# Down matrix of each expert loaded four neighbouring rows a partition, gate and up products read with a stride of four columns

## The chip, the cores and the metric

The kernel runs on one core of one Trainium2 chip. The metric is the device time of one execution in microseconds (us). Everything is in float32. "The span" is the time from the first to the last instruction of the profiled execution.

## The reference

The kernel computes two blocks one after the other on 256 tokens of width 1024 (272 rows with 16 meta tokens in the first layer). The first block has two layers, and each of these ends in a mixture of experts. That part is what the change touches:

```
def expert_block(args):
    xb, e = args
    hb = jax.nn.silu(xb @ w_gate[e]) * (xb @ w_up[e])
    return hb @ w_down[e]
```

There are 32 experts in each of the two layers; a token goes to two of them. `w_gate[e]` and `w_up[e]` are 1024 x 512, `w_down[e]` is 512 x 1024, so each of the three matrices is 2 MB and an expert is 6 MB. The second block (a state-space mixer, an MLP, attention, a second MLP) is not touched.

## The kernel before

**Experts.** Each layer's mixture of experts (`moe(l)`) runs over all 32 experts in order, with 32 token slots for each. For one expert TensorE does, in this order: `gate_up` (line 722), the weighing-in of the expert before (lines 751 and 755), a transpose of the hidden values (line 916), in some experts a `dispatch` of tokens for the next group of four experts (line 742) and in the first layer some preparation for the state-space mixer, and `down` (line 734). ScalarE applies silu (line 1435) and copies the transposed hidden values (line 1440); VectorE multiplies (line 2005) and copies the result out (line 2011).

**`gate_up`.** The stationary operand is a 128 x 32 slice of the tokens, and the moving operand is the weight. For each of the 8 slices `k` of the width, four matmuls with q = 0..3 write four groups of 32 partitions of one PSUM bank; each streams 256 columns, 128 of gate and 128 of up: columns 128q to 128q+127 of both. The profile counts two instructions for a float32 matmul, so 64 for a `gate_up`, in 16 sets of four. After silu, product and transpose, the 128 x 128 tile `hidT` holds for each q the hidden values of group q, with the hidden index on the partitions.

**`down`.** For each of 4 slices k, `hidT[:, 32k:32k+32]` is stationary, and row slice k of the down matrix is moving, in four column groups. Slice k of the down matrix must hold on partition p the row that belongs to hidden value p of group k: before the change this is row 128k + p.

**Loads.** The weights stream through `ring`, six slots of 16 KB a partition. All loads are issued by the sync engine (SP) in one order written out by hand: the three matrices of an expert after those of the one before, each as soon as its slot is free, which is when `gate_up` or `down` of the expert that held it is done. Two experts are in the ring at a time (slots in two sets of three, `expert_order` says in which order the three go); the third expert of each layer (`EXTRA`) goes to a part of `work`. In `load` (line 463 issues) gate and up are read as `"(p k) n -> p (k n)"`: partition p gets 8 neighbouring rows, one piece of 16 KB. Down is read as `"(q p) n -> p q n"`: partition p gets rows p, 128+p, 256+p, 384+p, four pieces of 4 KB:

```
if kind == "down":
    src = src.rearrange("(q p) n -> p q n", p=P)
else:
    src = src.rearrange("(p k) n -> p (k n)", k=DC)
```

TensorE waits before `gate_up` for the loads of gate and up, and before `down` for that of down. A second pass for overfull experts (`sp.Fori(1, rounds)`) has the same two forms.

**Around it.** Before the first mixture comes the recurrent mixer, between the two the short convolution (projections at lines 673 and 681, rows out at line 699), after the second everything of the second block.

Of the kernel before, what the change touches and what calls it, by code (L numbers as in the profile page):

```python
# [26 lines left out]
P = 128  # L27
D = 1024
DC = D // P
# [43 lines left out]
def first_and_second_block(nc, a, out):  # L73
# [4 lines left out]
    with ctx:  # L78
        def sb(name, shape, dt=F32):
            return ctx.enter_context(nc.sbuf_tensor(name, shape, dt))  # L80
# [52 lines left out]
        def S(name):  # L133

            name = shared.get(name, name)
            if name not in sems:
                sems[name] = nc.alloc_semaphore(name)
            return sems[name]

        def nth(name, count):  # L140

            return S(name), base.get(name, 0) + count


        ring = sb("ring", [P, NSLOT, SLOT])
# [133 lines left out]
        for name, _, over in plan:  # L279
            if name.startswith("experts"):  # L280
                place_experts(int(name[-1]))
            else:
                s = at % NSLOT
# [151 lines left out]
        @block.sync  # L435
        def _(sp):
            def slot_free(when):

                if when:
                    sp.wait_ge(*nth(when[0], when[1]))  # L440

            def load_experts(l, name):
                w = {"gate": a["moe_w_gate"][l], "up": a["moe_w_up"][l], "down": a["moe_w_down"][l]}

                def load(e, kind):

                    s = expert_slots[l, e, kind]
                    src = w[kind][e]
                    if kind == "down":
                        src = src.rearrange("(q p) n -> p q n", p=P)  # L450
                    else:
                        src = src.rearrange("(p k) n -> p (k n)", k=DC)
                    if s is not None:
                        dst = ring[:, s, :]
                        slot_free(expert_free[l, e, kind])
                        done = loaded[s]
                    elif kind == "down":
                        dst, done = extra_down[l], S("extra_down")
                    else:
                        dst, done = extra_gu[l][:, SLOT * (kind == "up"):SLOT * (kind == "up") + SLOT], S(f"extra_gu{l}")  # L460
                    if kind == "down":
                        dst = dst.rearrange("p (q n) -> p q n", q=4)
                    sp.dma_start(dst, src).then_inc(done, 16)

                for kind in expert_order[l, 0]:
                    load(0, kind)
                if l == 0:
                    sp.wait_ge(*nth("lru_z", DC))
                else:
                    sp.wait_ge(*nth("tabs_stored", 48))  # L470
                for kind in ("gate", "up"):
                    load(EXTRA, kind)
                for kind in expert_order[l, 1]:
                    load(1, kind)
                if l == 0:
                    sp.wait_ge(*nth("mix0_mixed", 3))
                load(EXTRA, "down")
                for e in range(EXTRA + 1, NE):
                    for kind in expert_order[l, (e - 1) % 2]:
                        load(e, kind)  # L480

                sp.wait_ge(*nth(f"rounds_known{l}", 1))
                rounds = sp.value_load(rounds_i[0:1, l:l + 1], min_val=1, max_val=MAX_ROUNDS)
                with sp.If(rounds > 1):
                    sp.wait_ge(*nth(f"down{l}", NE))
                    with sp.Fori(1, rounds) as r:
                        with sp.Fori(0, NE) as e:
                            n = (r - 1) * NE + e
                            sp.wait_ge(*nth(f"more_slots{l}", n + 1))
                            for kind, s in (("gate", 0), ("up", 1), ("down", 2)):  # L490
                                src = w[kind][e]
                                if kind == "down":
                                    src = src.rearrange("(q p) n -> p q n", p=P)
                                    dst = ring[:, s, :].rearrange("p (q n) -> p q n", q=4)
                                else:
                                    src = src.rearrange("(p k) n -> p (k n)", k=DC)
                                    dst = ring[:, s, :]
                                sp.dma_start(dst, src).then_inc(S(f"more_loaded{l}"), 16)
                        sp.wait_ge(*nth(f"more_used{l}", r * NE))
                        sp.sem_inc(S("more_rounds"), 1)  # L500
                sp.end_ifs()


            for b, (t0, n) in enumerate(BLOCKS):
                src = a["meta_tokens"] if b == 0 else a["x"][0, t0 - NMETA:t0 - NMETA + n, :]
                sp.dma_start(hres[0:n, b, :], src).then_inc(S(f"x_loaded{b}"), 16)
            sp.dma_start(ring[:, place["lru_x0"], :].rearrange("p (k n) -> p k n", k=DC), plan[0][1])\
                .then_inc(loaded[place["lru_x0"]], 16)
            vec = [(a["lru_conv_w"][0], 4), (a["lru_conv_b"], 1), (a["lru_b_a"], 1), (a["lru_b_i"], 1),
                   (a["lru_lambda"], 1), (a["sc_conv_w"][0], 3), (a["ssm_d_2"], 1),  # L510
                   (a["ln_g"][0, 1:2], 1), (a["ln_b"][0, 1:2], 1)]
            r = 0
            for src, n in vec:
                sp.dma_start(rowb[r:r + n, :], src).then_inc(S("vectors_loaded"), 16)
                r += n
            for i, w in enumerate((a["lru_w_a"][0], a["lru_w_i"][0])):
                for j in range(2):
                    sp.dma_start(w_gates[64 * j:64 * j + 64, i],
                                   w.rearrange("(m j) d e -> j d m e", j=2)[j]).then_inc(S("gates_loaded"), 16)
            names = [entry[0] for entry in plan]  # L520
            for name, src, _ in plan[1:]:
                if name in ("experts0", "experts1"):
                    load_experts(int(name[-1]), name)
                    continue
                s = place[name]
                slot_free(free_when[name])
                n = 1
                for x in src.shape[1:]:
                    n *= x
                dst = ring[:, s, 0:n]  # L530
                if len(src.shape) == 3:
                    dst = dst.rearrange("p (k n) -> p k n", k=src.shape[1])
                sp.dma_start(dst, src).then_inc(loaded[s], 16)

            for b in (1, 2):
                sp.wait_ge(*nth("mlp1_normed", b))
                t0 = BLOCKS[b][0] - NMETA
                sp.dma_start(out[0, t0:t0 + P, :], hres[:, b, :]).then_inc(S("stored"), 16)
            sp.wait_ge(*nth("stored", 32))
# [112 lines left out]
        def _(pe):  # L652
# [65 lines left out]
            def gate_up(x, bank, gu, k0=0, k1=DC):  # L718

                for k in range(k0, k1):  # L720
                    for q in range(4):
                        mm = pe.matmul(ps[32 * q:32 * q + 32, bank, 0:256].rearrange("p (u n) -> p u n", u=2),  # L722
                                       x[:, k, :], gu[:, k, :, P * q:P * q + P], start=(k == 0), stop=(k == DC - 1))
                return mm

            def pair(g):
# [82 lines left out]
            def moe(l):  # L809
# [76 lines left out]
                for e in range(NE):  # L886
# [13 lines left out]
                    if e == 0:  # L900
                        gate_up(x, 4 + b, gu, 0, 4)
                        pe.wait_ge(*nth(f"xT_ready{l}", 2))
                        gate_up(x, 4 + b, gu, 4, DC).then_inc(S(f"gate_up{l}"), 1)
                        turn_choices()
                    else:
                        gate_up(x, 4 + b, gu).then_inc(S(f"gate_up{l}"), 1)
# [95 lines left out]
            for j in range(2):  # L1002
                slot_wait(pe, f"lru_out{j}")
                w = slot_view(f"lru_out{j}", 4, D)
                for hf in range(2):
                    for q in range(4):
                        if hf == 0:
                            pe.wait_ge(*nth("lru_z", 4 * j + q + 1))
                        mm = pe.matmul(ps[32 * q:32 * q + 32, 2 + hf, :], lru_y[:, 4 * j + q, 0:32], w[:, q, 512 * hf:512 * hf + 512],
                                       start=(j == 0), stop=(j == 1), skip_group_check=True)  # L1010
# [40 lines left out]
            for m in range(1, DC):  # L1051
                for i, kind in enumerate(("cg", "v", "bg")):
# [6 lines left out]
                    t0, n = (t_first, TC) if kind != "bg" else (NMETA, SEQ)  # L1059
# [92 lines left out]
            for m in range(DC):  # L1152
                if m >= 2:
                    pe.wait_ge(*nth("glu_done", m - 1))
                for k0, k1 in (((0, 4), (4, DC)) if m == 0 else ((0, DC),)):
                    pe.wait_ge(*nth("s5_g", 1 if k1 == 4 else 2))
                    for i, kind in enumerate("vg"):
# [4 lines left out]
                        for k in range(k0, k1):  # L1162
                            mm = pe.matmul(ps[:, 2 * (m % 2) + i, 0:SEQ], w[:, k, P * (m % 4):P * (m % 4) + P], s5_g[:, k, :],  # L1163
                                           start=(k == 0), stop=(k == DC - 1))
# [29 lines left out]
            for b in range(2):  # L1194
                transposes("mlp0", [1, 2], "mlp0_normed", only=b)
                pe.wait_ge(*nth("mlp0_hT", 2 * b + 2))
                for name, n, bank in (("kv_a", KVL + ROPE, 2), ("q_a", QL, 4)):
                    slot_wait(pe, name)
                    w = slot_view(name, DC, n)
                    for k in range(DC):  # L1200
                        mm = pe.matmul(ps[:, bank + b, 0:n], hT[:, k, NMETA + P * b:NMETA + P * b + P], w[:, k, :],
                                       start=(k == 0), stop=(k == DC - 1))
# [11 lines left out]
            for h in range(HEADS):  # L1214
                for k in range(2):
                    mm = pe.matmul(ps[:, 2 + h // 2, SEQ * (h % 2):SEQ * (h % 2) + SEQ], wkv[:, k, h, 0:NOPE], ckvT[:, k, :],
                                   start=(k == 0), stop=(k == 1), skip_group_check=True)
# [20 lines left out]
            for b in range(2):  # L1238
                bank = (7, 0)[b]
                pe.wait_ge(*nth("values_out", b + 1))  # L1240
                for hh in range(2):
                    slot_wait(pe, f"q_b{hh}")
                    w = slot_view(f"q_b{hh}", 3, 768).rearrange("p k (h n) -> p k h n", h=4)
                    for k in range(3):
                        mm = pe.matmul(ps[:, bank, 256 * hh:256 * hh + 256].rearrange("p (h n) -> p h n", h=4),  # L1245
                                       cqT[:, k, P * b:P * b + P], w[:, k, :, NOPE:NOPE + ROPE],
                                       start=(k == 0), stop=(k == 2), skip_group_check=True)
# [18 lines left out]
            for h in range(HEADS):  # L1266
# [6 lines left out]
                for k in range(3):  # L1273
                    mm = pe.matmul(ps[:, 2 + h // 2, SEQ * (h % 2):SEQ * (h % 2) + SEQ], w[:, k, h % 4, 0:NOPE], cqT[:, k, :],  # L1274
                                   start=(k == 0), stop=(k == 2), skip_group_check=True)
# [1089 lines left out]
```

## Time and profile before

| | |
|---|---|
| median of 3 runs | 1934.17 us (1930.22 to 1934.27) |
| the profiled execution's own time | 1932.28 us |
| its span | 1930.5 us |
| granted TensorE clock, mean over the span | 0.917 |
| TensorE matmul busy | 1612.8 us (84%) |
| VectorE busy | 523.5 us (27%) |
| ScalarE busy | 212.9 us (11%) |
| DMA packets | 104440, of them 86908 under 8 KB |
| moved | 540.07 MB |

Busy times are sums over a whole execution of stages with different limits, so they don't say which engine sets the time of a stage. A matmul row with "x64" in a timeline is 64 instructions merged, and in brackets stands the idle time before it and what ended it.

### The profile page before, as it was taken

To read this page: it belongs to the slowest core of one execution; us is meant where nothing else is said; L and a number is where in the kernel's file an instruction comes from. 1 tells how busy PE (TensorE), PEld (TensorE's weight loads), DVE (VectorE), ACT (ScalarE), POOL (GpSimd) and SP (SyncE) were. 2 spreads that over 40 slices of the span, in tenths; PEclk is the share of its full clock that TensorE was granted. 3 is DMA by queue.
4 is the path that set the end of the run, shared out by engine and by line. 5 is a ranking of instruction groups with operands and counts; after the bars stand their busy time and mean duration, and the time that the engine had idled before them with its cause. 6 is when DMAs were issued, how large, how long until landed. Compare 5 with 4: busy or idle time off the path is not lost. (4 is left out here: it accounts for less than half of the span.)

```text
span 1930.5 us, 28771 instructions
## 1 busy us (share of the span) xinstructions
PE 1612.8 (84%) x12977; PEld 1072.4 (56%) x12977; DVE 523.5 (27%) x1257; ACT 212.9 (11%) x487; POOL 75.7 (4%) x97
## 2 busy tenths in 40 slices
PE   7999768888785999956547565799999998999998
PEld 5655445555453876534324332686886446588643
DVE  5752133433134214213211111621210022521002
ACT  2311011000101001000200000110110002311000
POOL 2000100000000100000000000320000010000000
PEclk9998889889888999978788787899999999999999
DMA  9356999999998845999999999644443424143410
GB/s 340 137 219 275 381 421 422 421 419 419 421 421 344 323 193 226 412 423 415 420 422 410 420 419 421 257 150 175 156 170 135 145 95 174 44 174 132 173 44 22
DMA packets 104440, 540.07 MB, mean 280 GB/s; under 512 B 7326, under 2 KB 9438, under 8 KB 86908
## 3 DMA queue, kind: packets, MB, share of 16 engines
q1 hardware_dynamic: 102428, 531.24, 69.0%
q0 software_dynamic: 1888, 6.95, 1.0%
q8 instruction: 105, 1.72, 0.4%
q14 instruction: 19, 0.16, 0.0%
HBM read 531.89 MB, written 6.29 MB: 279 GB/s over the span
## 5 line engine op out<-in xcount | busy, mean ns | idle before, releaser
L722 PE MATMUL ps<-ring,work 128*32 128x256 f32 x3968 | 290.3, 457 | 227.6 <-DMA ring<-in_moe_w_up 224.8
L722 PEld LDWEIGHTS ps<-ring,work 128*32 128x32 f32 x3968 | 160.0, 131 | 350.9 <-issue 304.4
L699 PE MATMUL ps<-ring,work 128*128 128x512 f32 x768 | 330.9, 592 | 0.0
L673 PE MATMUL ps<-hT,ring 128*128 128x256 f32 (+2 forms) x1488 | 329.3, 383 | 0.0
L673 PEld LDWEIGHTS ps<-hT,ring 128*128 128x128 f32 x1488 | 282.7, 191 | 45.2 <-issue 3.3
L699 PEld LDWEIGHTS ps<-ring,work 128*128 128x128 f32 x768 | 145.7, 190 | 182.2 <-issue 181.3
L734 PE MATMUL ps<-ring,multi 128*32 128x256 f32 x1984 | 127.3, 399 | 14.3 <-ACT multi L1440 12.1
L2005 DVE TENSOR_TENSOR rowb<-rowb,ps 128x128 f32<-128x128 f32 x64 | 18.4, 288 | 368.6 <-ACT rowb L1435 368.5
L2011 DVE COPY multi<-ps 128x256 f32<-128x256 f32 x64 | 27.2, 425 | 290.5 <-PE ps L734 290.4
L742 PE MATMUL ps<-rowb,hres 128*128 128x128 f32 (+1 forms) x640 | 103.5, 302 | 0.2 <-DVE rowb L1670 0.2
L742 PEld LDWEIGHTS ps<-rowb,hres 128*128 128x128 f32 (+1 forms) x640 | 85.5, 196 | 17.1 <-issue 1.8
L734 PEld LDWEIGHTS ps<-ring,multi 128*32 128x32 f32 x1984 | 60.4, 113 | 61.3 <-ACT multi L1440 19.0
L1435 ACT ACTIVATE rowb<-ps 128x128 f32<-128x128 f32 x64 | 17.8, 278 | 597.3 <-PE ps L722 597.3
L2247 DVE TENSOR_TENSOR work<-work 128x256 f32<-128x256 f32 x64 | 27.2, 425 | 192.9 <-ACT work L1546 192.9
L1655 DVE SCALAR_TENSOR_TENSOR tmp_a<-hres,ps 128x1024 f32<-128x1024 f32 (+1 forms) x7 | 8.5, 1219 | 248.2 <-PE ps L699 237.3
L751 PE MATMUL ps<-multi,tmp_a 32*128 32x256 f32 x1024 | 73.3, 400 | 1.1 <-DVE multi L2011 1.1
L751 PEld LDWEIGHTS ps<-multi,tmp_a 32*128 32x128 f32 x1024 | 46.2, 184 | 29.0 <-issue 25.5
L1163 PE MATMUL ps<-work,ring 128*128 128x256 f32 x256 | 55.5, 379 | 0.0
L1163 PEld LDWEIGHTS ps<-work,ring 128*128 128x128 f32 x256 | 48.6, 190 | 7.0 <-issue 0.4
L681 PE MATMUL ps<-hT,ring 128*128 128x128 f32 (+1 forms) x352 | 42.5, 283 | 5.6 <-ACT hT L1346 4.1
L681 PEld LDWEIGHTS ps<-hT,ring 128*128 128x128 f32 x352 | 41.5, 199 | 6.7 <-issue 5.7
L1546 ACT ACTIVATE work<-ps 128x256 f32<-128x256 f32 x64 | 24.6, 384 | 184.7 <-PE ps L673 171.9
(449 smaller groups left out, 1256.3 us busy)
## 6 DMA issues: line engine op xcount, KB each, us to landing
ring<-in_moe_w_gate SPq DMA_DIRECT2D x62, 2048.0 KB, 19.0
ring<-in_moe_w_up SPq DMA_DIRECT2D x62, 2048.0 KB, 23.6
ring<-in_moe_w_down SPq DMA_DIRECT2D x62, 2048.0 KB, 21.4
ring<-in_w_ff SPq DMA_DIRECT2D x32, 2048.0 KB, 8.1
ring<-in_sc_w_in SPq DMA_DIRECT2D x6, 2048.0 KB, 17.8
ring<-in_lru_w_in SPq DMA_DIRECT2D x4, 2048.0 KB, 15.8
ring<-in_ssm_w_glu SPq DMA_DIRECT2D x4, 2048.0 KB, 18.8
ring<-in_lru_w_out SPq DMA_DIRECT2D x2, 2048.0 KB, 19.8
```

What stands on the lines that cost most here:

```text
L673: mm = pe.matmul(ps[:, bank, 0:n], w[:, k, P * c:P * c + P], hT[:, k, t0:t0 + n], start=(k == 0), stop=(k == DC - 1))
L681: mm = pe.matmul(ps[:, bank, at:at + n], w[:, k, P * c:P * c + P], hT[:, k, t0:t0 + n], start=(k == 0), stop=(k == DC - 1))
L699: mm = pe.matmul(ps[0:m, 2 + 2 * b + hf, :], left[:, kk, t0:t0 + m], w[:, k, 512 * hf:512 * hf + 512], start=(kk == 0), stop=(kk == 4 * la ...
L722: mm = pe.matmul(ps[32 * q:32 * q + 32, bank, 0:256].rearrange("p (u n) -> p u n", u=2), x[:, k, :], gu[:, k, :, P * q:P * q + P], start=( ...
L734: mm = pe.matmul(ps[32 * q:32 * q + 32, bank, 0:256], hT_[:, 32 * k:32 * k + 32], w[:, k, 256 * q:256 * q + 256], start=(k == 0), stop=(k ...
L742: mm = pe.matmul(ps[:, bank, width * (k - k0):width * (k - k0) + width], hres[0:m, b, P * k:P * k + P], one_hot[0:m, i, 0:width], start=(i ...
L751: mm = pe.matmul(ps[:, q, SEQ * (b - 1):SEQ * b], w[r, t0:t0 + P], y[r, :], start=(first and b == 1), stop=False, skip_group_check=True)
L1163: mm = pe.matmul(ps[:, 2 * (m % 2) + i, 0:SEQ], w[:, k, P * (m % 4):P * (m % 4) + P], s5_g[:, k, :], start=(k == 0), stop=(k == DC - 1))
L1546: A(ff[:, c, :], ps[:, ff_bank(c), 0:SEQ], ACT.Relu).then_inc(S(f"ff_relu{layer}"), 1)
L2005: V.tensor_tensor(hid[b], silu[b], ps[:, 4 + b, P:2 * P], ALU.mult).then_inc(S(f"hid_ready{l}"), 1)
L2011: V.tensor_copy(y_out[b], ps[:, 4 + b, 0:256]).then_inc(S(f"y_ready{l}"), 1)
L2247: V.tensor_tensor(ff[:, c, :], ff[:, c, :], ff[:, c, :], ALU.mult).then_inc(S(f"ff_sq{layer}"), 1)
```

## The change

The down matrix is read as `"(p r) n -> p (r n)"`: partition p gets the four neighbouring rows 4p to 4p+3, one piece of 16 KB. Slice r of the slot then holds on partition p row 4p + r. So that the hidden values match, group q of `gate_up` takes columns q, 4+q, 8+q, ... (every fourth) of gate and of up, in place of 128 neighbouring ones. The number of matmuls, their sizes, the order of the loads and all waits are the same; `down` is unchanged.

```
@@ load_experts / load
                     if kind == "down":
-                        src = src.rearrange("(q p) n -> p q n", p=P)
+                        src = src.rearrange("(p r) n -> p (r n)", r=4)
...
-                    if kind == "down":
-                        dst = dst.rearrange("p (q n) -> p q n", q=4)
                     sp.dma_start(dst, src).then_inc(done, 16)
@@ the pass for overfull experts
                                 if kind == "down":
-                                    src = src.rearrange("(q p) n -> p q n", p=P)
-                                    dst = ring[:, s, :].rearrange("p (q n) -> p q n", q=4)
+                                    src = src.rearrange("(p r) n -> p (r n)", r=4)
+                                    dst = ring[:, s, :]
@@ gate_up
                         mm = pe.matmul(ps[32 * q:32 * q + 32, bank, 0:256].rearrange("p (u n) -> p u n", u=2),
-                                       x[:, k, :], gu[:, k, :, P * q:P * q + P], start=(k == 0), stop=(k == DC - 1))
+                                       x[:, k, :], gu[:, k].rearrange("p u (n r) -> p u r n", r=4)[:, :, q, :],
+                                       start=(k == 0), stop=(k == DC - 1))
```

## Rows read from the trace of the kernel before

**Rows 1.** The page, the span in 40 slices.

```profile
PE   7999768888785999956547565799999998999998
...
PEclk9998889889888999978788787899999999999999
DMA  9356999999998845999999999644443424143410
GB/s 340 137 219 275 381 421 422 421 419 419 421 421 344 323 193 226 412 423 415 420 422 410 420 419 421 257 150 175 156 170 135 145 95 174 44 174 132 173 44 22
```

**Rows 2.** Windows: busy time of each engine, clock, DMA share, GB/s.

```profile
core 0: us, PE busy (x) PEld busy (x) DVE busy (x) ACT busy (x) POOL busy (x), PEclk, DMA share, GB/s
216.00:604.00 388.00, 299.00 (x3483) 187.12 (x3484) 127.42 (x345) 36.41 (x88) 0.00 (x0) 0.87 1.01 419
772.00:1196.00 424.00, 258.06 (x3552) 156.13 (x3552) 85.91 (x208) 32.99 (x77) 3.62 (x5) 0.80 1.01 418
152.00:216.00 64.00, 59.41 (x738) 36.89 (x737) 17.54 (x51) 8.15 (x19) 8.50 (x12) 0.92 0.88 329
```

**Rows 3.** Waits of TensorE, 216 to 604, then 772 to 1196: us, times, longest.

```profile
PE ps L722 <- DMA ring<-in_moe_w_up: 64.5, 16, 7.4
...
PE ps L722 <- DMA ring<-in_moe_w_up: 154.8, 16, 13.3
```

**Rows 4.** Timeline of TensorE at four places: start, us, instructions.

```profile
216.31 3.22 PE L734 MATMUL ps<-ring,multi 128*32 128x256 f32 x32 [2.16 <-DMA ring<-in_moe_w_down]
226.96 5.36 PE L722 MATMUL ps<-ring,work 128*32 128x256 f32 x64 [7.43 <-DMA ring<-in_moe_w_up]
...
604.01 6.26 PE L722 MATMUL ps<-ring,work 128*32 128x256 f32 x64 [5.61 <-DMA ring<-in_moe_w_up]
...
803.36 5.35 PE L722 MATMUL ps<-ring,work 128*32 128x256 f32 x64 [3.80 <-DMA ring<-in_moe_w_up]
...
1195.99 5.53 PE L722 MATMUL ps<-ring,work 128*32 128x256 f32 x64 [12.69 <-DMA ring<-in_moe_w_up]
...
1205.78 3.66 PE L722 MATMUL ps<-ring,work 128*32 128x256 f32 x64 [0.62 <-DVE multi L2011]
```

**Rows 5.** DMA, 216 to 604: packets, and down issues with us to landing.

```profile
DMA packets 21029, 162.64 MB, mean 419 GB/s; under 512 B 1239, under 2 KB 1239, under 8 KB 14388
...
ring<-in_moe_w_down SPq DMA_DIRECT2D x25, 2048.0 KB, 23.4
```

**Rows 6.** The same view, 772 to 1196.

```profile
DMA packets 22981, 177.29 MB, mean 418 GB/s; under 512 B 1408, under 2 KB 1408, under 8 KB 15744
```

**Rows 7.** The same view, 6 us each from 1125 and 824.

```profile
DMA packets 170, 2.52 MB, mean 421 GB/s; under 512 B 16, under 2 KB 16, under 8 KB 16
...
DMA packets 175, 2.61 MB, mean 434 GB/s; under 512 B 16, under 2 KB 16, under 8 KB 16
```

**Rows 8.** The same view, 6 us each from 846 and 1114.

```profile
DMA packets 569, 2.36 MB, mean 394 GB/s; under 512 B 19, under 2 KB 19, under 8 KB 560
...
DMA packets 607, 2.41 MB, mean 402 GB/s; under 512 B 18, under 2 KB 18, under 8 KB 607
```

**Rows 9.** Timeline, one warm gate_up and what follows on TensorE.

```profile
441.20 3.66 PE L722 MATMUL ps<-ring,work 128*32 128x256 f32 x64
```

**Rows 10.** Line 722, instructions: ns min/median/max.

```profile
L722 PE MATMUL ps<-ring,work x3968: 376/379/636, 152.6 to 1209.1; 128*32 128x256 f32 x199
```

**Rows 11.** Lines 773 and 767, weight loads: ns min/median/max.

```profile
L773 PEld LDWEIGHTS ps<-ident,work x32: 182/202/205, 303.0 to 328.4; 64*128 64x128 f32 x32
...
L767 PEld LDWEIGHTS ps<-ident,work x6: 137/139/139, 300.6 to 300.9; 64*128 64x128 f32 x6
```

**Rows 12.** Weight loads: line 722 (ns min/median/max) and line 699 (busy us, mean ns).

```profile
L722 PEld LDWEIGHTS ps<-ring,work x3968: 106/110/178, 152.6 to 1208.8; 128*32 128x32 f32 x199
...
L699 PEld LDWEIGHTS ps<-ring,work 128*128 128x128 f32 x768 | 145.7, 190 | 182.2 <-issue 181.3
```

**Rows 13.** Groups by form, line 673: busy us, mean ns.

```profile
L673 PE MATMUL ps<-hT,ring 128*128 128x256 f32 x1008 | 219.0, 379 | 0.0
```

## The prediction

> **What bounds the kernel now.** I read the page's 40 slices first [rows 1]. In slices 5 to 11 and 16 to 24 the DMA row is at 9 with 410 to 425 GB/s, while PE is at 5 to 8: those are the two mixtures of experts. Elsewhere PE is at 9 and DMA far from full. So the change, which touches only the experts, meets two stretches in which the transfers look like the bound.
>
> The waits say so too. TensorE's first wait for an expert load in the first mixture ends at 216.31, its last at 604.01 [rows 4]; between these it waits 16 times for a gate/up pair, 64.5 us in all [rows 3]. In the second mixture the DMA is full from 772 and the last wait for a load ends at 1195.99 [rows 2, 4]; 154.8 us of waits lie between [rows 3]. Both stretches, 388 and 424 us, show a DMA share of 1.01 [rows 2]: there is never a hole in the stream. The queue is deep as well: a down load lands 23.4 us after its issue [rows 5], though alone it takes 2.097 MB / 0.419 = 5.0 us, so four to five loads are outstanding. The time of these two stretches is therefore bytes over rate: 162.64 MB is 25.9 experts of 6.29 MB, 177.29 MB is 28.2 [rows 5, 6]. TensorE only decides the start (152 to 216, where it is busy 59.4 of 64 us and the DMA share is 0.88 [rows 2]) and the tail behind the last load.
>
> **Edit 1, the down load.** A partition's piece of the down matrix grows from 4 KB to 16 KB, the size that gate and up already have. In the trace loads are so long that 6 us windows catch one kind alone. Eight windows in the second mixture with hardly a packet under 8 KB move 421 to 434 GB/s; their mean is 426 (the lowest and the highest stand in [rows 7]). Five windows in which nearly all packets are under 8 KB (down loads) move 394 to 402, mean 400 (again the lowest and the highest in [rows 8]). For 2.097 MB that is 4.92 and 5.24 us, 0.32 us less for a down load. A check by the whole stretch: with a third of the bytes at 400, the mean of 419 or 418 [rows 2] wants 429 or 428 for the other two thirds (3/419 = 1/400 + 2/429), and then a down load is 0.34 to 0.35 us shorter. I take 0.33. The ends are the windows' own: 421 against 402 gives 0.24, 434 against 394 gives 0.49.
>
> How many count: the loads that pass in the full stretches, 26 in the first and 28 in the second, 54 of 64. The others lie where TensorE sets the time and are worth nothing, since a free slot and not the transfer starts the next load there. So 54 x 0.33 = 17.8 us, with ends of 54 x 0.24 = 13 and 54 x 0.49 = 26. The other way to the same sum: 388 x (1 - 419/428) + 424 x (1 - 418/428) = 8.2 + 9.9 = 18.1.
>
> The Trainium skill has a rule that would give less. "DMA: Bandwidth & Descriptors", section "Specifications", asks only for 512 B a piece for the full rate, and its section "Why small descriptors are slow (HBM only)" prices a packet at about 3 extra cycles beside one for each 32 B. An estimate from that page: 4 x (128 + 3) against 512 + 3 cycles is 1.7%, 0.09 us a down load, 5 us in all. The windows show 6%, and the measurement decides.
>
> Does the gain stay? While TensorE waits for 64.5 and 154.8 us [rows 3], it can follow a stream that is 8 and 10 us shorter. Behind each stretch TensorE is the bound [rows 1], and its work there moves forward with its start. Semaphores, slots and the order of issue are the same; the SP queue issues as many DMAs as before.
>
> **Edit 2, the stride.** `gate_up` streams as many columns with as many instructions; what changes is that neighbouring columns of a moving operand are 16 B apart and not 4. Now a `gate_up` at full clock is 3.66 us for 64 instructions [rows 9], four side by side: 16 sets of 229 ns, with 379 ns for each instruction [rows 10]. No matmul in this trace streams a moving operand with such a stride. The nearest row is a weight load: line 773 reads columns 64 B apart and takes 202 ns, line 767 the same shape with neighbouring columns 139 ns [rows 11]. The stride costs that load 63 ns on 128 columns, 0.49 ns a column.
>
> The bounds: below, nothing (a stride can't bring columns sooner than neighbours come). Above, 256 x 0.49 = 126 ns a set, 16 x 126 = 2.0 us an expert, if the four streams of a set pay together, and four times that, 8.1 us, if they pay in turn. Which end is nearer? What counts is whether strided columns come as fast as a matmul takes them, 229 / 256 = 0.89 ns each. Plain weight loads take 110 ns for 32 columns and 190 for 128 [rows 12]: 0.83 ns a column and 83 ns of start-up. With that start-up, line 767 reads 56 ns long, 0.44 ns a column, and line 773 119 ns, 0.93 ns a column. That is almost exactly the matmul's pace: over a set 256 x (0.93 - 0.89) = 10 ns, 0.16 us an expert. So I take nothing for one stream. Whether four at once get this each, no row shows. With neighbouring columns they do: a set of four takes 229 ns, a single matmul of as many columns 219.0 us / 1008 = 217 ns [rows 13]. I take nothing for four as well, and this is the weakest step.
>
> The Trainium skill speaks against it: "Advanced Engine Details and Errata", section "SBUF Cachelines", says that SBUF is read in lines of 16 B and that an access which goes to a new line each time is penalised; at least two hits on a line are needed. With a stride of 16 B every column is a new line. The rule has no price; what it would do here is priced from rows as the first and the second rival below.
>
> **The sum.** 1932.3 (the profiled execution) - 17.8 = 1914.5. The runs' median is 1.9 us above that execution, so 1916.4. Forecast: 1916 us.
>
> **The rivals.**
>
> *A partial stride cost, up to 2.0 us an expert.* In the full stretches it is mostly hidden: 26 x 2.0 = 52 is less than 64.5 of waits, 28 x 2.0 = 56 less than 154.8. It shows where TensorE leads: six experts at the start of the first mixture (12 us), two at the start of the second (4), one `gate_up` behind the last wait at 604 (2) and two behind that at 1196 (4). Together 22: 1938 us. With 1 us an expert it is 1927.
>
> *TensorE becomes the bound (this is the slower case).* Place: `gate_up`; mechanism: the strided streams cannot be fed at the matmul's pace. It decides once the extra time of an expert passes the waits divided by the experts, less the stream's own gain: (64.5 - 8)/26 = 2.2 us in the first mixture, (154.8 - 10)/28 = 5.2 in the second. If the streams are served in two turns and a set takes double, 16 x 0.229 = +3.7 us: 26 x (3.7 - 2.2) = 39, starts 8 x 3.7 = 30, tails 3 x 3.7 = 11, with the second mixture hidden: +80, from 1916 to 1996; as a TensorE with fewer idle stretches has a higher granted clock than 0.87 [rows 2], I say 1965 to 1995. If four streams are served in turn, +8.1 us: 26 x 5.9 + 28 x 2.9 + 8 x 8.1 + 3 x 8.1 = 153 + 81 + 65 + 24 = 323, that is 2240. For it: line 773's weight loads, which do take longer with a stride. Against: the 0.93 ns a column that they come to, and the set of four that costs no more than one matmul today.
>
> *The piece's size does not matter, and the 400 against 426 comes from something else* (the down matrix's rows in memory, what lies behind it in the queue). Then nothing moves: 1934. Against it: the difference is in each of the windows.
>
> **Chances.** Stride free and the gain as summed 0.55; partial cost 0.15; sets doubled 0.12; served in turn 0.13; no gain from the pieces 0.05. What a measurement of this kernel tells from no change is about 0.2%, 4 us: 1930 to 1938. Faster takes all of the first and a third of the second, 0.60; same takes the last and 0.07 of the second, 0.12; slower the other 0.03 of the second and both forms of TensorE as the bound, 0.28. The likeliest case's own range is 1908 (26 us, the upper end) to 1922 (13 us, with a spread of 1 or 2 us). The range for 8 in 10 must reach into the doubled case: 0.55 + 0.15 + 0.05 + a part of 0.12, so up to 1975.
>
> **What would show each step.** DMA packets fall by 64 x 384 = 24576 to about 79,860, and those under 8 KB by 32768 to about 54,140. The two stretches show 426 to 429 GB/s and are 8 and 10 us shorter. Line 722 keeps a median of 379 ns and a warm `gate_up` its 3.66 us: the stride is free. If a `gate_up` is longer, it tells which rival; if the wait for up in the first mixture falls from 64.5 us to near nothing and the DMA share below 1.0, TensorE has become the bound. If the packets fall but the rate stays at 419, the third rival holds. The prediction is wrong above all if the moving operand's stride costs more than 2 us an expert.

## The result, and the profile after

| | before | changed |
|---|---|---|
| median | 1934.22 us | 1963.18 us (1959.88 to 1964.07, 4 runs) |
| ratio | | 1.0156 (95% interval 1.0133 to 1.018) |
| the profiled execution | 1932.28 us | 1959.88 us, span 1958.2 |

The change costs 29 us where 18 us of gain were forecast. The time lies inside the stated range, but the kernel became slower where the forecast said faster.

The page of the changed kernel, counts and slices, against [rows 1]:

```profile
PE   7999999999997999977687777899999998999998
...
PEclk9999999999998999998898888899999999999999
DMA  9356899999998844899999999734434333243410
GB/s 340 139 207 258 336 426 427 426 426 413 419 427 352 324 197 186 367 398 415 424 412 408 406 410 426 299 131 172 165 137 172 104 133 141 75 161 140 171 44 21
DMA packets 79865, 540.07 MB, mean 276 GB/s; under 512 B 7327, under 2 KB 9439, under 8 KB 54141
```

The loads did what was said: 79865 packets and 54141 under 8 KB are the forecast counts. In the first mixture (slices 5 to 11) the rate is a little higher than before, 423 GB/s on average for 421. But PE is now at 9 through that whole mixture, and in the second (slices 17 to 24) the rate is lower than before in most slices.

Line 720 is `gate_up`, 722 before. Its instructions (ns min/median/max), then windows, as [rows 2]:

```profile
L720 PE MATMUL ps<-ring,work x3968: 610/632/669, 151.5 to 1235.8; 128*32 128x256 f32 x199
```

```profile
216.00:604.00 388.00, 368.70 (x3613) 181.84 (x3613) 127.44 (x348) 37.52 (x92) 0.00 (x0) 0.99 1.00 423
772.00:1196.00 424.00, 335.56 (x3475) 155.17 (x3473) 81.90 (x199) 34.69 (x78) 3.62 (x5) 0.90 0.95 397
```

A matmul instruction takes 632 ns against 379 in [rows 10], and TensorE is busy 369 of 388 us where it was 299. In the second mixture the DMA share is 0.95 and the rate 397 GB/s, against 1.01 and 418. TensorE's timeline there, two experts (against [rows 9]):

```profile
1096.53 7.46 PE L720 MATMUL ps<-ring,work 128*32 128x256 f32 x64 [8.27 <-DMA ring<-in_moe_w_up]
1103.92 1.15 PE L750 MATMUL ps<-multi,tmp_a 32*128 32x256 f32 x16
1105.00 0.33 PE L915 MATMUL ps<-ident,rowb 128*128 128x128 f32 x1
1105.16 1.95 PE L741 MATMUL ps<-rowb,hres 128*128 128x128 f32 x16
1107.04 1.93 PE L733 MATMUL ps<-ring,multi 128*32 128x256 f32 x32
1108.79 7.47 PE L720 MATMUL ps<-ring,work 128*32 128x256 f32 x64
...
1127.63 0.66 PE L720 MATMUL ps<-ring,work 128*32 128x256 f32 x4 [6.38 <-DMA ring<-in_moe_w_up]
```

A `gate_up` is 7.46 us, 465 ns a set of four, twice the 229 of before. Still TensorE waits 8.3 and 6.4 us for loads: it is no longer fed at full rate although it is the slower one. The sync queue at the same time shows why:

```profile
1084.68 0.33 SPq L461 DMA_DIRECT2D ring<-in_moe_w_gate  x1
1085.05 0.43 SPq L461 DMA_DIRECT2D ring<-in_moe_w_up  x1
1088.32 21.05 SPq L461 DMA_DIRECT2D ring<-in_moe_w_down  x2
1109.41 0.43 SPq L461 DMA_DIRECT2D ring<-in_moe_w_gate  x1
1109.88 0.43 SPq L461 DMA_DIRECT2D ring<-in_moe_w_up  x1
```

The third row merges two down loads, one at 1088.32 and one at 1109.0; nothing is issued between them. In the second mixture every other expert is loaded down first (`expert_order`), and its down slot is free only when the `down` of the expert two before is done, at 1108.97. Gate and up stand behind it, though their slots came free with the `gate_up` that ended at 1103.99. From the end of TensorE's wait (1096.53) to the end of `down` it is 12.4 us; in the kernel before, the same stretch is 10.1 us (1135.46 to 1145.53). The three loads still outstanding at 1096.53 (gate, up and down of the next expert, issued at 1084.68, 1085.05 and 1088.32) last some 14.7 us (3 x 2.097 MB at 427 GB/s), less the time that a new one needs to get going, so now the stream can run dry once in two experts. The DMA view of 1066 to 1128 (a slice is 1.55 us) has the hole at its 28th to 30th slice:

```profile
DMA  9999999999999999999999999994889899999999
GB/s 402 465 391 455 402 444 433 412 307 402 444 423 423 423 444 433 412 455 402 455 412 444 423 433 444 412 433 180 180 338 476 381 476 381 455 433 412 455 402 476
```

### The profile page after: what moved, and what is told of

It is laid out like the page before. It is cut to its first block and busy times, and to the rows that moved or that the text cites. A ratio compares the mean times of both kernels' runs of the same rounds, so it can differ in the third digit from the quotient of the medians.

```text
span 1958.2 us, 28771 instructions
## 1 busy us (share of the span) xinstructions
PE 1778.7 (91%) x12977; PEld 1061.0 (54%) x12977; DVE 524.5 (27%) x1257; ACT 212.8 (11%) x487; POOL 75.5 (4%) x97
## 2 busy tenths in 40 slices
DMA packets 79865, 540.07 MB, mean 276 GB/s; under 512 B 7327, under 2 KB 9439, under 8 KB 54141
## 5 line engine op out<-in xcount | busy, mean ns | idle before, releaser
L720 PE MATMUL ps<-ring,work 128*32 128x256 f32 x3968 | 462.1, 632 | 101.5 <-DMA ring<-in_moe_w_up 101.5
L720 PEld LDWEIGHTS ps<-ring,work 128*32 128x32 f32 x3968 | 152.6, 130 | 371.9 <-issue 367.2
L733 PE MATMUL ps<-ring,multi 128*32 128x256 f32 x1984 | 121.7, 386 | 12.5 <-ACT multi L1439 12.5
L1434 ACT ACTIVATE rowb<-ps 128x128 f32<-128x128 f32 x64 | 17.8, 278 | 642.4 <-PE ps L720 642.4
```

The lines of the kernel that those rows point to most:

```text
L733: mm = pe.matmul(ps[32 * q:32 * q + 32, bank, 0:256], hT_[:, 32 * k:32 * k + 32], w[:, k, 256 * q:256 * q + 256], start=(k == 0), stop=(k ...
```

## The experiments

Edits are against the kernel before unless another is named. Ratios are against the kernel before, run beside them on the same chip.

**The two parts alone.** `e1_loads_only` is the changed kernel with this line put back, `e2_stride_only` the kernel before with the changed one:

```
-  x[:, k, :], gu[:, k].rearrange("p u (n r) -> p u r n", r=4)[:, :, q, :], start=..., stop=...)
+  x[:, k, :], gu[:, k, :, P * q:P * q + P], start=..., stop=...)
```

> The loads of the down matrix in pieces of 16 KB, and gate/up products that read neighbouring columns as before (the hidden values then meet the wrong rows of the down matrix, so what is computed differs in that). Theory: the pieces are worth what the windows said, 54 loads x 0.33 us = 18 us, so about 1916 us, with 427 GB/s in both mixtures and a gate_up of 3.66 us. Rival: the piece's size is worth nothing by itself, 1934 us.

Measured: 1922.3 us, ratio 0.9951 (0.9932 to 0.997). A gain of 9 us (0.49%, by the ratio 9.5): clear of noise, and about half of the forecast. The wrong hidden values of this kernel and the next can change the routing of the second layer, but the work stayed the same: 12977 matmul instructions in both, as before.

> The loads as before in pieces of 4 KB, and gate/up products with the stride of four columns (again hidden values and rows don't match). Theory: the stride doubles a set of four matmuls (229 to 465 ns) and costs some 45 us in all with the loads of the change; with slower loads TensorE has more slack in the mixtures, so 1963 to 1975 us. If the load's gain and the stride's cost simply add, 1963 + 18 = 1981. Rival: part of the doubling comes from the loads (a full-rate stream into the same memory), then a gate_up is shorter than 7.4 us here.

Measured: 1969.28 us, ratio 1.0195 (1.017 to 1.022), and a `gate_up` is 7.4 us here too. The stride costs 38 us with the old loads. With the new ones it costs 1.0156 / 0.9951, 2.06% or 40 us. The two parts add within the intervals (0.9951 x 1.0195 = 1.0145), and the doubling does not come from the new loads. The additive 1981 us of the expectation was too high because it took the loads' gain as 18 us.

**Half the way.** `e3_pairs` loads two neighbouring rows a partition and strides by two columns:

```
-  src = src.rearrange("(q p) n -> p q n", p=P)
+  src = src.rearrange("(h p r) n -> p h (r n)", p=P, r=2)
...
-  gu[:, k, :, P * q:P * q + P]
+  gu[:, k].rearrange("p u (h n r) -> p u h r n", h=2, r=2)[:, :, q // 2, q % 2, :]
```

> Two neighbouring rows a partition, pieces of 8 KB, and gate/up products with a stride of two columns (8 B). Theory (what costs is that each column lies in a new line of 16 B, two columns a line are enough): a gate_up stays at 3.66 us, the pieces give two thirds of the gain, about 12 us, so 1922 us. Rival (any stride costs, in proportion to the bytes passed over): a set at about 340 to 460 ns, 1940 to 1965 us.

Measured: 1928.13 us, ratio 0.9984 (0.9967 to 1.0001). A `gate_up` takes 3.81 us against 3.64: a stride of 8 B costs 5%, not 100%. The time is 6 us above the 1922 expected, and the gain is not clear of its interval. Per load the pieces of 8 KB do bring about two thirds: the experts 7 to 10 of the first mixture follow each other in 14.90 us before, 14.75 here and 14.68 in `e1_loads_only`.

**What a stride costs, by itself.** `e5_probes` adds twelve groups of 64 products behind the last stage, one source line each (`R` runs twice over the 8 slices k and the four q), such as

```
+  for k, q in R:
+      pe.matmul(pout(q), px[:, k, :], strided(k, 4, q), start=True, stop=True)
```

> The kernel before with twelve groups of 64 matmuls (128 instructions each, 256 moving float32 columns) behind its last stage: four column groups side by side with stride 1; all four on the same neighbouring columns; stride 2; stride 3; stride 4; stride 4 with all four on the same columns; stride 4 with the four in different parts of memory; two column groups with stride 4; one column group with stride 4; a full 128-column array with stride 1, 2 and 4. Theory A (each stream pays a new 16 B line for each column, whatever the others do): a single stream with stride 4 is as slow as four, some 465 ns for two instructions against 434 and for a full array well above its 434 too. Theory B (four streams share the line reads): one or two streams with stride 4 cost nothing, 217 ns an instruction, and only four side by side pay; four on the same columns then pay less or the same, four in different places the same or more. Strides 2 and 3 lie between in both.

The timeline of TensorE behind the last stage (start, us; 128 instructions a row), where its granted clock is 1.00:

```profile
1937.47 7.08 PE L1335 MATMUL ps<-ring,hT 128*32 128x256 f32 x128
1944.37 7.50 PE L1337 MATMUL ps<-ring,hT 128*32 128x256 f32 x128
1951.67 11.27 PE L1339 MATMUL ps<-ring,hT 128*32 128x256 f32 x128
1962.67 14.81 PE L1341 MATMUL ps<-ring,hT 128*32 128x256 f32 x128
1977.18 14.82 PE L1343 MATMUL ps<-ring,hT 128*32 128x256 f32 x128
1991.70 14.85 PE L1345 MATMUL ps<-ring,hT 128*32 128x256 f32 x128
2006.29 29.29 PE L1347 MATMUL ps<-ring,hT 128*32 128x256 f32 x128
2035.39 58.02 PE L1349 MATMUL ps<-ring,hT 128*32 128x256 f32 x128
2093.34 27.89 PE L1352 MATMUL ps<-ring,hT 128*128 128x256 f32 x128
2121.07 29.15 PE L1354 MATMUL ps<-ring,hT 128*128 128x256 f32 x128
2150.06 58.11 PE L1356 MATMUL ps<-ring,hT 128*128 128x256 f32 x128
```

Lines 1335 to 1345 are four column groups side by side: stride 1 (all on the same columns), 2, 3, 4, 4 on the same columns, 4 in different parts of memory: 221, 234, 352, 463, 463, 464 ns a set. Line 1347 has two groups side by side, line 1349 one, both with stride 4: 458 and 453 ns for a step. Lines 1352 to 1356 fill the whole array with one stream: 218, 228 and 454 ns an instruction for stride 1, 2 and 4. So theory A holds: each stream pays for itself, at stride 4 an instruction takes 1.8 ns a column in place of 0.85, and it does not matter how many streams run beside it or where they read. Four streams side by side were never the risk.

**TensorE time without a strided read.** `e6_twice` is `e1_loads_only` with every product of `gate_up` issued twice.

```
+  for twice in range(2):
       for q in range(4):
-          mm = pe.matmul(..., start=(k == 0), stop=(k == DC - 1))
+          mm = pe.matmul(..., start=(k == 0 and twice == 0), stop=(k == DC - 1 and twice == 1))
```

> The loads of the change, gate/up products on neighbouring columns but every product issued twice and added twice (so the hidden values are other ones): a gate_up takes 7.3 us warm without any strided read. Theory (what the stride costs is TensorE time alone): near the changed kernel, 1958 to 1968 us. Rival (the strided reads also slow the loads or other engines' reads): clearly faster than the changed kernel, 1950 us or less.

Measured: 1986.57 us, ratio 1.028 (1.0246 to 1.0313), slower than the changed kernel and outside what either theory gave. Its `gate_up` at two places of the second mixture:

```profile
1080.97 9.71 PE L721 MATMUL ps<-ring,work 128*32 128x256 f32 x128 [6.79 <-DMA ring<-in_moe_w_up]
1094.14 7.09 PE L721 MATMUL ps<-ring,work 128*32 128x256 f32 x128
```

It takes 7.09 us warm (at the full granted clock) but 8.5 to 9.96 us after waits of 3.6 us and more, while the strided one takes 7.4 to 7.6 us in both cases. Of the 26 us between the two profiled executions 25 lie in the second mixture (481.1 us from the first `gate_up` to the last, against 456.0), where each longer `gate_up` behind a wait also holds up the queue longer. So the kernel is not faster without strided reads, but with this added cost it is no clean test of the rival. Other rows are: with strided reads `e7_order` (below) loads at 427 GB/s, the rate of `e1_loads_only` without them, and VectorE's multiplication and ScalarE's silu take 288 and 278 ns each before and in the changed kernel. By these rows the strided reads slow neither. The changed kernel behind the wait that ended at 1127.63, windows (columns as in [rows 2]):

```profile
1127.70:1131.00 3.30, 3.30 (x32) 1.50 (x36) 0.00 (x0) 0.00 (x0) 0.00 (x0) 0.50 1.04 447
1133.00:1135.00 2.00, 2.00 (x20) 0.53 (x12) 0.00 (x0) 0.00 (x0) 0.00 (x0) 1.00 0.98 418
```

and its weight loads there, one row a set:

```profile
1128.97 0.19 PEld L720 LDWEIGHTS ps<-ring,work 128*32 128x32 f32 x4 [0.26 <-issue]
1129.44 0.20 PEld L720 LDWEIGHTS ps<-ring,work 128*32 128x32 f32 x4 [0.27 <-issue]
1129.89 0.20 PEld L720 LDWEIGHTS ps<-ring,work 128*32 128x32 f32 x4 [0.26 <-issue]
...
1133.06 0.18 PEld L720 LDWEIGHTS ps<-ring,work 128*32 128x32 f32 x4 [0.28 <-issue]
1133.51 0.18 PEld L720 LDWEIGHTS ps<-ring,work 128*32 128x32 f32 x4 [0.28 <-issue]
```

At a granted clock of 0.50 (the 1.2 GHz level) the sets follow each other in 0.45 to 0.47 us, and from 1133, where it is 1.00, in 0.45. So the pace of a strided stream does not follow that clock. With neighbouring columns it is the clock that counts: the `gate_up` of before takes 3.66 us warm and 6.26 behind the wait that ended at 604.01 [rows 4, 9].

**The order of the queue.** `e7_order` is the changed kernel with one order for all experts:

```
-  for kind in expert_order[l, (e - 1) % 2]:
+  for kind in ("gate", "up", "down"):
```

(and the same for the experts 0 and 1).

> The changed kernel, with the loads of each expert issued as gate, up, down in both mixtures; in the second, every other expert had down, gate, up. Theory (the second mixture loses time because the load of down stands first in the queue and waits for the down product of the expert two before, while gate and up behind it have free slots): the holes in the stream go, the second mixture is 10 to 15 us shorter, 1948 to 1953 us. Rival (the second mixture is long because TensorE lacks time there): no change, 1963 us.

Measured: 1945.2 us, ratio 1.0067 (1.004 to 1.0094), so 0.9% or some 17 us less than the changed kernel, a little more than expected. The second mixture, from the first `gate_up` to the last, is 444.0 us long (772.28 to 1216.23) against 456.0 (772.90 to 1228.86). From 835 to 1200 its DMA view reads

```profile
DMA packets 10704, 155.88 MB, mean 427 GB/s; under 512 B 1189, under 2 KB 1189, under 8 KB 1189
```

and TensorE waits only 0 to 4.9 us for a load. With a strided `gate_up` of 7.4 us the stream is full all the same: past the start of the second mixture TensorE was not the bound, the order of the queue was.

**The order in the kernel before.** `e9_order_before` has the same edit in the kernel before.

> The kernel before with nothing changed but the order of issue: gate, up, down for every expert of both mixtures. Theory: in the second mixture of the kernel before, down at the head of the queue also left small holes in the stream; without them its last 24 experts come every 14.9 us in place of 15.1, so 3 to 6 us less in all, about 1927 us, and the even spacing shows what a piece of 4 KB costs: 14.88 us an expert against 14.68 with 16 KB. Rival: no holes before, 1932 us, and the spacing stays at 15.1, which would put the price of the 4 KB pieces at 0.4 us.

Measured: 1931.89 us, ratio 0.9996 (0.9981 to 1.0011): no gain that can be told from zero, though the interval would still allow 3.7 us. With a short `gate_up` the holes are small, 418 GB/s from 860 to 1150 against 421 here. Its even spacing does give the price of the pieces: mostly 14.90 us an expert where TensorE waits each time, against 14.68 in `e8_best`, and over 26 experts (812.25 to 1204.51, and 802.48 to 1188.91 there) 15.09 against 14.86 us on average. That is 0.22 us a down load.

**A version that beats both.** `e4_block_transpose` keeps the 16 KB loads and the products on neighbouring columns. The order of the hidden values is mended where it is cheap, on VectorE, whose transpose works in blocks of 32 x 32: block (q, r) of every fourth column goes to partitions 32q.. and columns 32r.., which is just what row 4p + r on partition p asks for. It takes the place of TensorE's transpose (line 916) and ScalarE's copy (line 1440):

```
+  V.transpose(out=hidT[b].rearrange("p (r t) -> p r t", r=4), in_=hid[b].rearrange("p (m r) -> p r m", r=4))
```

> Pieces of 16 KB, gate/up products on neighbouring columns, and the hidden values put in the order of the rows by VectorE: one transpose in blocks of 32 x 32 that reads every fourth column, in place of TensorE's transpose and ScalarE's copy. Theory: it keeps the whole gain of the loads, 1914 to 1916 us, and a gate_up of 3.66 us. Rival: the longer VectorE work or the strided read on VectorE delays down and with it the slots, so that it is above the kernel with the loads alone by more than 4 us.

Measured: 1915.88 us, ratio 0.9925 (0.9904 to 0.9947): 15 us under before, and 6 under the loads alone, though these two intervals overlap a little. `e8_best` adds the order of `e7_order`.

> Pieces of 16 KB, products on neighbouring columns, block transpose on VectorE, and the order gate, up, down for all experts. Theory: with a short gate_up the queue hardly runs dry, so the order is worth 0 to 5 us on top of the block transpose: 1911 to 1916 us, 0.990 of before. Rival: the order shortens the wait for gate and up of every other expert and brings nothing since the stream is full, 1916 us.

Measured: 1913.4 us, ratio 0.9903 (0.988 to 0.9925), 19 us under before. What the order adds to the block transpose is not clear of the intervals.

## Why the prediction was wrong, point by point

**The bound.** Right that both mixtures run at the rate of the loads, and that the rest is TensorE's. Wrong in "there is never a hole in the stream": a DMA share of 1.01 over 424 us hides holes of a microsecond. From 1086.5 the kernel before has one,

```profile
DMA packets 333, 1.30 MB, mean 325 GB/s; under 512 B 16, under 2 KB 16, under 8 KB 333
```

325 GB/s over 4 us, on a down load. In the second mixture two down loads follow each other in the queue and the second waits at its head, and the waits of TensorE there (16 for 28 experts, up to 13.3 us [rows 3]) were the sign of it: one expert of two waited long, the other hardly or not at all.

**Edit 1.** The mechanism was right, the term too large: 0.22 us a down load in place of 0.33, and 9.5 us in all in place of 17.8 (`e1_loads_only`); 54 x 0.22 would be 12. The windows that gave 400 GB/s for pieces of 4 KB [rows 8] were few and not typical: a window of 6 us with down loads alone needs two of them in a row, which only the second mixture has, and its second down load is the one that lies ahead of a hole. In `e9_order_before`, without such pairs, even windows of 4 us with at least 97% of their packets under 8 KB are rare from 860 to 1150: three, at 404, 414 and 417 GB/s. Holes are not the whole reason: in the first mixture such 4 us windows show about 400 as well (402 from 221.5 in `e9_order_before`), and why such windows price a down load higher than the spacing of the experts does stays open. The check by the stage means had the same fault, as it took the 400 for granted. Better was a long stretch: from 440 to 560, before and then `e1_loads_only`,

```profile
DMA packets 3521, 51.24 MB, mean 427 GB/s; under 512 B 393, under 2 KB 393, under 8 KB 393
```

427 against 420 GB/s, which is 14.73 against 14.98 us an expert. Besides, some experts of the first mixture do not wait for loads before or after, since the preparation for the state-space mixer falls on them. The estimate of 5 us from the Trainium skill's "DMA: Bandwidth & Descriptors", section "Why small descriptors are slow (HBM only)", was too low against the 9.5 us, the windows too high.

**Edit 2, the step that failed.** "I take nothing" was the weakest step, as it said, and it was wrong: the price is 236 ns a set (465 against 229; 242 in the probes), 3.8 us an expert at full clock, a doubling. The upper bound of 126 ns a set from line 773's weight loads did not bound it: those loads reach 0.93 ns a strided column, a float32 matmul instruction takes 1.8. A strided weight load is no measure for a strided moving operand; why the two differ no run shows. The Trainium skill was right in "Advanced Engine Details and Errata", section "SBUF Cachelines": an access that goes to a new line of 16 B each time is penalised, and two hits a line are needed. The probes agree: at stride 4, one column a line, an instruction takes 454 ns against 218, and at stride 2, two columns a line, 228. That rule deserved more than the 0.25 that the two rivals had together.

**The rival that came true, and its price.** TensorE's strided set doubled, the size that the second rival gave, though not by its mechanism: the streams are not served in two turns, since one alone is as slow. The time is 1963 where that rival summed to 1996 and said 1965 to 1995, and it lies elsewhere. That 1963 falls so near the lower end is luck: the first mixture lost far less than its sum, the second more. Against `e1_loads_only` (profiled spans 1958.2 and 1917.0, so 41 us) the parts are, from the starts of the first and the last `gate_up` of each mixture:

| | forecast if doubled | measured |
|---|---|---|
| first mixture | 39 + 22 | 457.5 - 445.8 = 11.7 us |
| second mixture | 8 + 4, else hidden | 456.0 - 435.4 = 20.6 us |
| before, between and behind | 7 | 8.9 us |

(The 4 and the 7 are the 11 us of the tails, as one of the three `gate_up` lies inside the second mixture.) In the first mixture nearly nothing was lost past its start: from expert 6 to expert 31 the changed kernel needs 372.5 us (236.53 to 609.00), `e1_loads_only` 371.9 (223.26 to 595.12) and the kernel before 377.1 (226.96 to 604.01). Two things that the sum left out made room. A strided `gate_up` costs the same at the low clock, where the old one already took 5 to 6.6 us behind most waits, so the true addition is less than 3.7 us for those behind a wait. And the busier TensorE is granted 0.99 in place of 0.87, which shortens its other products (`down` takes 386 ns an instruction on average for 399). The waits for loads fell from 64.5 us to

```profile
PE ps L720 <- DMA ring<-in_moe_w_up: 7.7, 4, 3.1
```

with the DMA share still at 1.00. In the second mixture the waits seemed to leave 5.2 us an expert, and the price was 20 us all the same: the wait of TensorE is no slack if the queue that would use it is stopped behind another wait. `e7_order` shows it, as it takes 12.0 us from that mixture with the stride in place; the 8.6 that are left are near the 8 that were forecast for its start. `e7_order` gains some 17 us in all; the 5 outside the second mixture can't be assigned with one profile of each, as executions differ by a few us.

**The other rivals.** "The piece's size does not matter" is out by `e1_loads_only`. "Served in turn" is out by the probes: one stream is as slow as four. "A partial cost up to 2.0 us" is out too, as it is 3.8.

## What to carry to other kernels

Put a permutation where columns are cheap to skip (here VectorE's transpose), and not on the moving operand of a matmul at a stride of 16 B: a float32 stream takes twice the time there, at 8 B 5% more. When a stage is bound by loads, read the issue queue too: a load that waits at its head for a late slot stops those behind it, and the slack that TensorE's waits show is then not there to be used. Take the price of a transfer from long stretches or from the spacing of steps that all wait, not from short windows that catch one kind alone.

## What the runs showed of the hardware that was not expected

A strided stream's pace does not follow TensorE's granted clock: a set of four took 0.45 to 0.47 us at 0.50 and 0.45 at 1.00. So a strided `gate_up` is only some 14% slower than the slowest plain one behind a wait (7.45 against 6.55 us, at 893.55 in the kernel before, granted 0.50 from there to 897) and twice as slow as a warm one (3.66). The cost is per stream and not shared: one group of 32 columns, two, four and the whole array all take 453 to 464 ns for 256 columns with stride 4. And a 32 x 32 block transpose on VectorE that reads every fourth column cost the chain no more than TensorE's transpose with ScalarE's copy; by the medians it was some 6 us of 1922 cheaper, which the intervals leave open.
